# Two decoder layers in float32: the GLA output norm ahead of the keys' evacuation, five homes for high halves, the low half of a weight awaited at the third pass, and tiles split earlier

## The reference

```
x <- LN(alpha * x + Mixer(x))            w_in (1024 x 3088), w_out (1024 x 1024)
x <- LN(alpha * x + MemXAttn(x, mem))    256 memory tokens, 4 heads of 256
x <- LN(alpha * x + FFN_l(x))            layer 0: SwiGLU, 2816 wide; layer 1: top 2 of 8 experts, 3584 wide
```

```
oc = gla_chunked(qc, kc, vc, log_a)
oc = rms_norm(oc, gla_g) * silu(gc)
o  = concatenate([oa, ob, oc]);  return o @ w_out
```

## Time and profile before

| | |
|---|---|
| median of 3 runs | 1790.13 us (1789.71 to 1792.11) |
| the profiled execution | 1789.71 us, of which the span is 1787.9 us |
| TensorE, matmuls | busy 1715.6 us, 96% of the span |
| VectorE | 1332.3 us, 75% |
| ScalarE | 1017.9 us, 57% |
| GpSimd | 22.2 us, 1% |
| DMA | 465.98 MB, mean 261 GB/s |
| DMA queue q1, hardware_dynamic | 200880 packets, 463.76 MB |
| expert loads | 336 of 1 MB, 5.5 us each from issue to landing (median) |
| granted TensorE clock | 0.985 of full speed over the span |

### The profile page before, as it was taken

The page is one execution under the profiler, slowest core; times in us unless marked ns, Lnnn a source line. Parts: engine busy times, 40 slices in busy tenths (PEclk is TensorE's granted clock), DMA queues, the critical chain, the costliest instruction groups (busy, mean ns, idle before and its releaser), DMA issues.

```text
span 1787.9 us, 21664 instructions
## 1 busy us (share of the span) xinstructions
PE 1715.6 (96%) x7978; PEld 1372.2 (77%) x7978; DVE 1332.3 (75%) x1229; ACT 1017.9 (57%) x895; POOL 22.2 (1%) x32
## 2 busy tenths in 40 slices
PE   7989999999899999989999999999999999999996
PEld 5845777888776568777888888888888888888884
DVE  4475756445554576579889899899898898998996
ACT  4344344334343534347677677777777776777772
POOL 0001000000000010000000000000000000000000
PEclk9999999999999999989999999999999999999998
DMA  8422435546543234389999999999999999999990
GB/s 286 176 71 95 165 118 176 182 137 212 188 142 140 95 118 142 125 309 354 365 348 366 344 361 369 340 365 372 338 366 354 351 373 341 363 371 336 367 370 35
DMA packets 206471, 465.98 MB, mean 261 GB/s; under 512 B 11952, under 2 KB 14544, under 8 KB 206416
## 3 DMA queue, kind: packets, MB, share of 16 engines
q1 hardware_dynamic: 200880, 463.76, 72.5%
q10 hardware_dynamic: 5536, 1.48, 0.4%
HBM read 464.16 MB, written 1.05 MB: 260 GB/s over the span
## 4 chain that ended last, share of the span: by engine, by line
PE 88%; DVE 6%; DMA 2%; ACT 2%; issue 1%; DVEq 0%; ACTq 0%; SPq 0%
PE ps L1549 19%; PE ps L2008 17%; PE ps L2010 17%; PE ps L2009 17%; PE ps L1577 4%; PE ps L1926 3%; PE ps L1985 2%; PE ps L1510 2%; PE ps L1994 1%; DVE w_lo L961 1%; DVE ring_r L949 1%; PE ps L1703 1%; PE ps L1758 1%; DMA ring<-in_xa_wq_dram 1%; PE ps L1826 1%
## 5 line engine op out<-in xcount | busy, mean ns | idle before, releaser
L961 DVE TENSOR_TENSOR w_lo<-ring,w_hi 128x2048 fp32r<-128x2048 f32 x336 | 768.1, 2290 | 112.5 <-ACT w_hi L630 109.7
L630 ACT CAST w_hi<-ring 128x2048 fp32r<-128x2048 f32 x336 | 641.9, 1911 | 277.4 <-PE ps L2010 263.9
L2008 PE MATMUL ps<-w_hi,xe_hi 128*128 128x512 f32 x896 | 353.2, 394 | 1.8 <-DVE w_lo L961 1.8
L2010 PE MATMUL ps<-w_hi,xe_lo 128*128 128x512 f32 x896 | 349.3, 390 | 0.0
L2009 PE MATMUL ps<-w_lo,xe_hi 128*128 128x512 f32 x896 | 348.7, 389 | 0.0
L2008 PEld LDWEIGHTS ps<-w_hi,xe_hi 128*128 128x128 f32 x896 | 168.3, 188 | 37.2 <-DVE w_lo L961 2.7
L2010 PEld LDWEIGHTS ps<-w_hi,xe_lo 128*128 128x128 f32 x896 | 168.2, 188 | 35.8
L1549 PE MATMUL ps<-ring_r,xT_r 128*128 128x512 f32 (+1 forms) x704 | 186.9, 394 | 8.0 <-DVE late_r L940 7.5
L2009 PEld LDWEIGHTS ps<-w_lo,xe_hi 128*128 128x128 f32 x896 | 168.4, 188 | 33.8
L2008 PE MATMUL ps<-w_hi,he_hi 128*128 128x512 f32 x448 | 178.2, 398 | 0.0
L2010 PE MATMUL ps<-w_hi,he_lo 128*128 128x512 f32 x448 | 174.8, 390 | 0.0
(11 more groups left out here) (266 smaller groups left out, 1772.0 us busy)
## 6 DMA issues: line engine op xcount, KB each, us to landing
ring<-in_moe_w_dram SPq DMA_DIRECT2D x336, 1024.0 KB, 5.5
ring<-in_ffd_w_dram SPq DMA_DIRECT2D x31, 1024.0 KB, 5.1
ring<-in_w_in_dram SPq DMA_DIRECT2D x24, 1024.0 KB, 5.2
ring<-in_xa_wkv_dram SPq DMA_DIRECT2D x16, 1024.0 KB, 5.0
ring<-in_w_out_dram SPq DMA_DIRECT2D x8, 1024.0 KB, 5.1
ring<-in_xa_wq_dram SPq DMA_DIRECT2D x8, 1024.0 KB, 5.1
ring<-in_xa_wo_dram SPq DMA_DIRECT2D x8, 1024.0 KB, 5.1
ring<-in_ffd_w_dram SPq DMA_DIRECT2D x4, 512.0 KB, 3.6
```

Of the source, the lines that this page charges most:

```text
L630: act.copy(w_hi[:, q % SPLIT_SLOTS, :], ring[:, q % RAW_SLOTS, :]).then_inc(hi_ready, 1)
L961: dve.tensor_tensor(w_lo[:, q % SPLIT_SLOTS, :], ring[:, q % RAW_SLOTS, :], w_hi[:, q % SPLIT_SLOTS, :].bitcast(F32), ALU.subtract).then_i ...
L2008: pe.matmul(ps[:, bank, :], x_hi, hi[:, c, cols], start=first, stop=False)
L2010: return pe.matmul(ps[:, bank, :], x_lo, hi[:, c, cols], start=False, stop=last)
```

## The change

It has these parts:

1. `HIGH_SLOTS` is 5: ring slot 6 (`spare`) becomes a fifth home of high halves. The rank weights and their two parts, which lay there, get buffers of their own (`w_rank`, `wr_split`), and the program's `dynamic_dma_scratch_size` is set to 4096 bytes, which leaves room for them. The w2 panels still end with four halves gone through by tile (`LAST_SLOTS`).
2. `HI_LO` becomes (high, high), (low of x, high), (high, low of the weight). TensorE waits for the high half at the first pass and for the low half at the third (`part_ready`), for tile 0; `raw_ready` is the wait for the memory's key and value weights, as before.
3. At the start both splitting engines do tile 0 and two halves, then tile 1 and two halves, and TensorE waits for tile 1 after the first pair of panels on tile 0.
4. VectorE does the GLA norm of both tiles, with the multiplications, ahead of the kT copies. One low half that stood ahead of the multiplications comes behind the split of tile 0, and the last two come behind that of tile 1.
5. At the border TensorE transposes tile 0 of the new x ahead of the last w2 half on tile 1; ScalarE evacuates it with two high halves still to make; VectorE makes its low part and one low half ahead of tile 1's residual.

```diff
-HIGH_SLOTS = 4
+HIGH_SLOTS = 5
+LAST_SLOTS = 4
-            homes[l, n, g] = ("o_tok", "dec_late", "ring", "qk")[turn % HIGH_SLOTS]
+            homes[l, n, g] = ("spare", "o_tok", "dec_late", "ring", "qk")[turn % HIGH_SLOTS]
-        w_rank = spare[:, 12 * P:14 * P].rearrange("p (l c r) -> p l c r", l=DEPTH, c=KC)
+        w_rank = sb("w_rank", [P, DEPTH, KC, CR])
+        wr_split = sb("wr_split", [P, 2, KC, CR], F32R)
...
             # ScalarE, and VectorE alike with split_low
-            turn_split(TURN["x0"])
+            turn_split(TURN["x0"], (0,))
-            split_high(4)
+            split_high(2)
+            turn_split(TURN["x0"], (1,))
+            split_high(2)
...
             # ScalarE, border
-                    split_high(2 * W2_P - 1)
+                    split_high(2 * W2_P - 1 - 2)
                     turn_split(TURN["x3", l], (0,))
+                    split_high(2)
...
             # VectorE, GLA norm
                     norm_of(slice(4 * t, 4 * t + 4), CV)
-                    if t == 0:
-                        turn(TURN["k", l], kT)
-                split_low(1)
                 for t in range(T):
...
                     dve.sem_inc(mixed, 1)
-                for t in range(T):
-                    turn_split(TURN["mix", l], (t,))
-                    split_low(1)
+                turn(TURN["k", l], kT)
+                turn_split(TURN["mix", l], (0,))
+                split_low(1)
+                turn_split(TURN["mix", l], (1,))
+                split_low(2)
...
             # VectorE, border
                             split_low(1)
-                    turn_split(TURN["x3", l], (0,))
-                    split_low(3)
+                            turn_split(TURN["x3", l], (0,))
+                            split_low(1)
+                    split_low(2)
...
-            HI_LO = ((0, 0), (0, 1), (1, 0))
+            HI_LO = ((0, 0), (1, 0), (0, 1))
+            def part_ready(l, n, g, m):
+                if m == 0:
+                    pe.wait_ge(dense_hi, SPLIT_AT[l, n, g] + 1)
+                if m == 2:
+                    pe.wait_ge(dense_lo, SPLIT_AT[l, n, g] + 1)
-                        if t == 0 and step % 12 == 0:
-                            half_ready(l, n, g)
+                        if t == 0 and c == 0:
+                            part_ready(l, n, g, m)
-            for t in range(T):
-                turned(TURN["x0"], t)
                 if l == 0:
+                    turned(TURN["x0"], 0)
                     gemm_pair(l, 0, 0)
+                    turned(TURN["x0"], 1)
-                    by_tile = last + 1 - HIGH_SLOTS
+                    by_tile = last + 1 - LAST_SLOTS
+                            if t == 1 and i == last:
+                                turn_x("x3", 3 * l + 2, 0)
                             ins = w2(i, t)
-                    turn_x("x3", 3 * l + 2, 0)
-    nc = bacc.Bacc("TRN2", target_bir_lowering=False, num_devices=1)
+    nc = bacc.Bacc("TRN2", target_bir_lowering=False, num_devices=1, dynamic_dma_scratch_size=4096)
```

More of the change, by code:

```diff
@@ L251, in bass_decoder @@
         stx = spare[:, 8 * P:12 * P].rearrange("p (b h s) -> p b h s", b=2, h=2)
-        high = {"ring": ring_r[:, DENSE_SLOTS, :], "o_tok": late_r[:, 8192:10240], "dec_late": late_r[:, 12288:14336],
+        high = {"spare": ring_r[:, RAW_SLOTS - 1, :], "ring": ring_r[:, DENSE_SLOTS, :], "o_tok": late_r[:, 8192:10240], "dec_late": late_r[:, 12288:14336],
                 "qk": qk_r[:, :, :, :].rearrange("p m n s -> p (m n s)"), "tr": late_r[:, 2048:4096],
@@ L273, in bass_decoder @@
         rt = s4[:, 0, :, 0:T * 24 * 4].rearrange("p n (t k) -> p n t k", t=T)
-        wr_hi, wr_lo = (ring_r[:, RAW_SLOTS - 1, m * KC * CR:(m + 1) * KC * CR].rearrange("p (c r) -> p c r", c=KC)
-                        for m in range(2))
+        wr_split = sb("wr_split", [P, 2, KC, CR], F32R)
+        wr_hi, wr_lo = (wr_split[:, m, :, :] for m in range(2))
         rankT = spare[0:CR, 14 * P:16 * P]
@@ L962, in low @@
                                   w_hi[:, q % SPLIT_SLOTS, :].bitcast(F32), ALU.subtract).then_inc(lo_ready, 1)
-            turn_split(TURN["x0"])
-            split_low(4)
+            turn_split(TURN["x0"], (0,))
+            split_low(2)
+            turn_split(TURN["x0"], (1,))
+            split_low(2)
             dve.wait_ge(pos_in, 32)
@@ L1516, in turned, with raw_ready @@
                     pe.wait_ge(tp_taken[b], m + 1)
-            HI_LO = ((0, 0), (0, 1), (1, 0))
-            def half_ready(l, n, g):
-                if (l, n, g) in SPLIT_AT:
+            HI_LO = ((0, 0), (1, 0), (0, 1))
+            def raw_ready(l, n, g):
+                at = HALF_AT[l, n, g]
+                pe.wait_ge(dense_in[at % DENSE_SLOTS], 16 * (at // DENSE_SLOTS + 1))
+            def part_ready(l, n, g, m):
+                if m == 0:
+                    pe.wait_ge(dense_hi, SPLIT_AT[l, n, g] + 1)
+                if m == 2:
                     pe.wait_ge(dense_lo, SPLIT_AT[l, n, g] + 1)
-                else:
-                    at = HALF_AT[l, n, g]
-                    pe.wait_ge(dense_in[at % DENSE_SLOTS], 16 * (at // DENSE_SLOTS + 1))
             STEPS = 24
@@ L1575, in piece @@
                     if c == 0 and t == 0:
-                        half_ready(l, IN_P + n, g)
+                        raw_ready(l, IN_P + n, g)
                     ins = pe.matmul(ps[:, piece_bank(i), :], memT[:, k, t * P:(t + 1) * P],
@@ L1923, in w2 @@
                             for m, (p, q) in enumerate(HI_LO):
+                                if t == 0 and col == 0:
+                                    part_ready(l, n, g, m)
                                 for c in range(2):
```

## The result

| | before | after |
|---|---|---|
| median of 4 runs, side by side | 1790.59 us (1789.71 to 1792.11) | 1768.39 us (1766.63 to 1771.28) |
| ratio, with its 95% interval | | 0.9877 [0.9861, 0.9893] |
| profiled execution / its span | 1789.71 / 1787.9 us | 1766.63 / 1764.8 us |
| TensorE busy with matmuls | 1715.6 us | 1707.9 us |
| mean granted clock | 0.985 | 0.990 |

The change makes the kernel 22.2 us (1.2%) faster; 17.3 had been forecast. 1768.4 lies in the range, 4.4 us under the predicted 1772.8.

The account below looks back on a forecast made before the run. The prediction took TensorE, busy 96% of the span, as the bound. Start 3.9, norms 5.0 and 4.6, border 3.8 sum to 17.3 us: 1789.7 - 17.3 + 0.4 = 1772.8 us, range 1768.0 to 1777.5.

Parts of the forecast that it names:

- What bounds the kernel: Whole kernel: TensorE is busy 96% of the span; a microsecond counts only if TensorE idles or runs at half clock.
- the four places named: Where TensorE waits: the start, the norm of layer 0 and of layer 1, and the border between the layers; 17.3 us together.
- The sign as it was written: Forecast is wrong if border-to-end is not as long as before, or VectorE reaches tile 1's norm over 13 us after w2.
- The start, 3.9: First weights: TensorE starts at about 12.4, not 16.3, with the low half awaited at the third pass; 3.9 us at most.
- Rival 2: Start: its 3.9 us are given back if the sixth half lands when it did and TensorE waits; 1776.7 us, chance 0.12.
- The norm, 5.0 and 4.6: GLA norm, layers 0 and 1: TensorE's wait goes and the output projection starts sooner; 5.0 and 4.6 us, bounds 3.3 to 5.5.
- the 0.4 for slow first projection matmuls: Part of each norm term: the output projection's first four matmuls take 1.1 us, not 1.49.
- The border, 3.8: Between the layers: transposing and splitting x earlier gains 6.2 us less 2.4 for the clock, so 3.8; bounds 3.2 and 6.2.
- the clock's fall, priced at 2.4: Border: the new stretch is longer than two in the trace, so the clock falls; price 2.4, the middle of 1.8 and 3.0.
- rival 1: Border: the clock holds, gaining 6.2 us in place of 3.8; 1770.4 us, chance 0.24.
- At nothing: Parts costed at zero: the fifth home of high halves, the new order of passes, the rank weights' own buffers, the scratch.
- Rival 3: Loads: the smaller scratch slows every load, shown by expert loads landing above 5.8 us; 15% gives 1823 us, chance 0.02.

Follow-up runs that it names:

- e5: The changed kernel with four homes of high halves again in place of five, all else kept; 1769.02 us.
- e7: The changed kernel unaltered, measured and profiled once more; 1769.32 us.
- e8: The changed kernel with one of VectorE's two low halves ahead of the last hidden chunk's product, which w2 waits for, moved behind it; 1764.48 us.
- e9: e8 with, at the entry of the experts, VectorE's take of tile 1's transposes put ahead of a low half; 1763.88 us.
- e3: The kernel before with only the start's order changed: tile 0 and two halves, then tile 1 and two halves; 1789.54 us.
- e4: The kernel before with only the order of the three passes changed, high half awaited at the first and low half at the third; 1788.00 us.
- e1: The kernel before with only the GLA norm's order changed: both tiles' norm and multiplications ahead of the kT copies, low halves behind; 1779.52 us.
- e2: The kernel before with only the border's order changed, keeping four homes and the old order of passes; 1783.76 us.
- e6: The kernel before with the scratch of 4096 bytes and the rank weights in buffers of their own; 1791.13 us, ratio 1.0002.
- e11: The changed kernel with all three edits, those of e8, e9 and e10; 1767.24 us.
- e10: The changed kernel with the second layer's rank weight issued 50 us later; 1767.96 us.

## Why the prediction was right, and where it was off

**What bounds the kernel, and the sign: right.** All that was gained was gained at the four places named and at w2's entry. From layer 1's output projection to the end the stretch is as long as before (23.4 and 23.1 us of lead). The sign as it was written, that the stretch from the border to the end must be as long as before, contradicted the sum's own 4.6 for layer 1's norm; that stretch is 4.7 us shorter.

**The start, 3.9: right in its steps, wrong in its upper bound.** TensorE began at 12.63 (12.4 forecast), a gain of 3.7, and 4.5 by the memory's transposes, where 3.9 was called the most: the slow stretch behind it was shorter (96 matmuls in 24.35 us, 25.11 before), which the term left out. ScalarE's first cast began at 10.58, where I had it at 10.4. **Rival 2**, given a chance of 0.12, came true in part: an idle of 1.0 to 2.0 us at 38.7 to 39.8 in three of five profiles (e5, e7, e8; not the kernel after, nor e9). It was no weight transfer that was late, as that rival had it, but ScalarE, held by the issue of transfers, which takes longer in the changed kernel (5.7 to 8.4 us, 5.0 to 5.5 before). The row that I read ("ScalarE is free for it at 36") had the time and not its cause, and took it as unchanged. e3 and e4 together are 3.4 us.

**The norm, 5.0 and 4.6: right, 5.4 and 5.0 measured**, and 10.9 for both in e1. The wait went, as forecast. Undersized was the tail: I took 3.7 us for the transposes and key matmuls from the rows' lengths; by starts it is 3.07 (bounds of 5.5 had said so). Wrong in its reason was the 0.4 for slow first projection matmuls: they take 1.33 us by starts at full clock as well (1.00 at 183 to 185; listed with 1.50 us, and with 1.49 before, where the clock was at 1.00 again from 193 on), so their slowness was never the clock's. What the clock gave back was ahead of them, in the transposes (3.06 us by starts before, 1.75 after) and the four key matmuls (1.91 and 1.32): the granted clock lacked 1.71 us there before, at 189 to 193, and nothing after.

**The border, 3.8: the mis-sized term.** The shown profile gained 7.1, above the upper bound of 6.2; e2 gained 6.7. Two steps of it failed. First, the sum without clock: w2 and x's split left no wait at all (470.13 follows 469.64), where 0.3 was forecast; tile 1's norm ended 12.5 us behind w2's end (482.6) and not 13.2, so that TensorE's stop was 1.19 and not 1.75 us; and from tile 1's transposes to its first matmul it took 2.70 and not 2.9. With 11.4 and not 11.2 us for the 48 matmuls between, these make 0.9, and 6.2 becomes 7.1. Second, the clock's fall, priced at 2.4. In the shown profile it didn't come: **rival 1** (6.2, chance 0.24) is what this execution did. In most it does:

| stretch without weight matmuls on TensorE | fell / profiles | lost when it fell |
|---|---|---|
| eight transposes, 1.87 us idle (tile 1 in the kernel before, e1 to e4, e6) | 0 / 6 | |
| eight transposes, 2.5 to 2.8 us idle (w2's entry, all but e8, e9, e11) | 8 / 10 | 1.7, once 3.4 us |
| 1.1 to 1.2 us idle, eight transposes, 1.6 us idle (border: after, e5, e7 to e11) | 6 / 7 | 1.7 (four), 3.4 (two) |

So the step "the new stretch is longer than both, and the clock falls" holds as a statement of likelihood, six times in seven, and the price of 2.4 lies between the 1.7 and the 3.4 that were found. The six falls cost 2.3 us in the mean; with one, the border gives about 7.1 - 2.3 = 4.8, where 3.8 was said. The profile in which it held is of the same program as e7's, where 3.4 us were lost: the comparison with the two stretches gave the direction, and no certainty. What in the stretch decides it, the idle or the transposes, no run shows, since eight transposes are in each of the three.

**w2's entry: not in the sum.** I had its row and took it as unchanged. In both profiles of the changed kernel the clock held there, 1.6 us that nobody had counted; in e5 and e10, whose edits leave the work ahead of it in the same order, it fell, and in all six profiles of the kernel before and its variants too. I take it as a chance of the execution, but no program shows both outcomes at this place, so that a part of the change in it isn't excluded. With these it stands thus: forecast 17.3; border +3.3, w2's entry +1.6, start +0.6, norms +0.8, the rest -0.5: 23.1, the profile's gain. The medians' gain is 22.2. The border's usual fall and the start's idle take from it, but how often they come in the executions without a profile isn't on record. That the forecast of 17.3 came as near as it did is in part luck: the clock's fall at the border, which was counted on, did not come in the profiled execution, and the 1.6 us at w2's entry, which nobody counted, did.

**At nothing: right.** Fifth home (e5, 1769.02 beside 1769.32), buffers and scratch (e6, 1.0002). Rival 3 is excluded. What was to show it, a landing time above 5.8 us, was badly chosen: four profiles have 6.1 to 6.6, kernels of the old scratch size among them, and none is slower for it. The new order of passes isn't quite free: 96 matmuls take 22.34 to 22.37 us in the feed-forward of layer 0, 22.27 before, some 0.3 us over all of it (9.9 to 9.7 in the table of leads). With the order of the passes alone (e4) they take 22.31, so about half of that is the order; the rest is unexplained. Against rival 3 the prediction had the queue of the loads (q1, `hardware_dynamic` on the page, 463.76 of the 465.98 MB); that such a queue is spared by a smaller scratch was the author's assumption. What e6 shows is the result for this kernel: with 4096 bytes of scratch and the same 463.76 MB on q1 it is no slower, ratio 1.0002 [0.9992, 1.0012].

## What to carry to other kernels

When TensorE waits for a producer at a stage's end, list what that producer does in the last few microseconds and ask of each item whether its reader is already waiting; here, putting off one or two conversions of 2.3 us that were wanted 5 us later bought 5 us at each of the two norms and, with x transposed and split sooner, about 7 at the border; the same look at w2's entry removed 2.6 us of idle. Cost a wait at its idle plus the slow stretch behind it, but treat the slow stretch as a chance (here 0, 1.7 or 3.4 us behind the same stops of the border), read from several profiles of one program. Here ScalarE paid for the transfers that it issued, 5.0 to 8.4 us for two at 26 us and 0.37 for one at 78.7: look at what stands behind an issue in its queue. The fastest versions here were e8 and e9, 1764.48 and 1763.88 us.

## What was not expected of the hardware

- The same program had its clock hold in one execution and fall in the next behind the same idle: at the border, 1.19 and 1.61 us of it in the kernel after (held) and in e7 (fell). At w2's entry it held after 2.57 and 2.67 us and fell after 2.50, 2.60 and 2.70, there in different programs. When it fell, windows of 1 us show a loss of 1.71 us or a multiple of it (3.42, and 6.83 or 8.53 behind the entry of the experts).
- The issue of two transfers of rank weights from ScalarE took 5.7, 6.7, 7.3, 7.8 or 8.4 us in the changed kernel's executions, 5.0 to 5.5 in the kernel before's, nearly all of it the second one (5.1 to 7.2 us; 0.6 the first in four of five). The same second issue took 0.37 us when it stood 50 us later.
- The changed kernel's profile shows full clock up to 736 us (except that it misses the slow start), and then 8.5 us lost at 736 to 754, behind the entry of the experts. The kernel before lost 6.8 there (762 to 777), and its variants 8.5. It is the largest loss left in the records while TensorE has work; the half clock of the last 17 us lies almost wholly behind its last matmul (1749.39).
